# Two feed-forwards' products down in seven block products for each pair of weight chunks, products up in one bank

## The reference

```python
# first block: D_FF = 2816
h = rms_norm(x, ffn_norm_g[l])
g = jnp.einsum('bld,df->blf', h, w_gate[l])
u = jnp.einsum('bld,df->blf', h, w_up[l])
x = x + jnp.einsum('blf,fd->bld', jax.nn.silu(g) * u, w_down[l])
# second block: D_FF_2 = 4096; here the result is normed before it is added to x
relu(h @ w_up_2) ** 2 @ w_down_2
```

## Time and profile before

| | before |
|---|---|
| median of 3 runs | 761.1 us (760.95 to 761.15) |
| profiled execution's span | 759.5 us (mean granted clock 0.997) |
| PE busy | 741.9 us (98%), 4410 matmuls |
| DVE busy | 462.9 us (61%) |
| ACT busy | 373.5 us (49%) |
| POOL busy | 112.7 us (15%) |
| transferred | 130.46 MB, mean 172 GB/s |

### The profile page before, as it was taken

How to read it: one execution, slowest core, us unless ns; L and a number is a source line. 1 busy time by engine, 2 the same in 40 slices (tenths; PEclk the granted TensorE clock), 3 DMA queues, 4 the chain that set the end, 5 groups by cost and what they waited for, 6 DMA issues and landing times.

```text
span 759.5 us, 11083 instructions
## 1 busy us (share of the span) xinstructions
PE 741.9 (98%) x4410; PEld 643.3 (85%) x4410; DVE 462.9 (61%) x643; ACT 373.5 (49%) x535; POOL 112.7 (15%) x138
## 2 busy tenths in 40 slices
PE   6999999999999999999999999999999999999996
PEld 5877778999999999888888888888778899988895
DVE  5898696765555555465746656674848754455433
ACT  6656654654444444275434524663338644344431
POOL 3857540100000000002100000000302111001110
PEclk9999999999999999999999999999999999999998
DMA  9642152786656676355625543474535765655511
GB/s 326 213 127 83 46 173 78 239 285 211 207 188 190 188 227 203 112 174 187 195 84 192 193 139 112 127 262 136 170 102 201 255 197 188 202 187 184 188 45 55
DMA packets 70179, 130.46 MB, mean 172 GB/s; under 512 B 5312, under 2 KB 29072, under 8 KB 70128
## 3 DMA queue, kind: packets, MB, share of 16 engines
q1 hardware_dynamic: 68144, 125.00, 51.8%
q0 software_dynamic: 1552, 4.20, 1.8%
q10 hardware_dynamic: 432, 0.56, 0.2%
HBM read 128.62 MB, written 1.05 MB: 171 GB/s over the span
## 4 chain that ended last, share of the span: by engine, by line
PE 92%; DVE 3%; DMA 2%; issue 1%; ACT 1%; SPq 0%; DVEq 0%; ACTq 0%
PE psum L450 40%; PE psum L885 29%; PE psum L503 11%; PE psum L927 2%; DMA w_raw<-in_w_in 2%; PE psum L677 1%; PE psum L1012 1%; PE psum L598 1%; PE psum L543 1%; PE psum L628 1%; PE psum L1044 1%; DMA w_raw<-in_w_out 1%; PE psum L579 1%; DVE w_lo L1893 1%; PE psum L649 1%
## 5 line engine op out<-in xcount | busy, mean ns | idle before, releaser
L1893 DVE TENSOR_TENSOR w_lo<-w_raw,w_hi 128x1024 fp32r<-128x1024 f32 x225 | 275.3, 1235 | 153.2 <-ACT w_hi L1270 152.5
L1270 ACT ACTIVATE w_hi<-w_raw 128x1024 fp32r<-128x1024 f32 x231 | 241.4, 1059 | 181.3 <-PE psum L885 77.3
L885 PE MATMUL psum<-h_hi,w_hi 128*128 128x256 f32 x608 | 170.3, 284 | 0.6 <-issue 0.6
L885 PE MATMUL psum<-h_hi,w_lo 128*128 128x256 f32 x608 | 169.5, 283 | 0.0
L885 PE MATMUL psum<-h_lo,w_hi 128*128 128x256 f32 x608 | 161.8, 281 | 0.0
L885 PEld LDWEIGHTS psum<-h_hi,w_hi 128*128 128x128 f32 x608 | 114.7, 189 | 1.7 <-issue 0.7
L885 PEld LDWEIGHTS psum<-h_hi,w_lo 128*128 128x128 f32 x608 | 114.4, 188 | 0.0
L885 PEld LDWEIGHTS psum<-h_lo,w_hi 128*128 128x128 f32 x608 | 111.1, 189 | 0.7
L450 PE MATMUL psum<-w_hi,h_hi 128*128 128x512 f32 (+1 forms) x240 | 94.0, 392 | 0.0
L450 PE MATMUL psum<-w_hi,h_lo 128*128 128x512 f32 (+1 forms) x240 | 93.0, 387 | 0.0
L450 PE MATMUL psum<-w_lo,h_hi 128*128 128x512 f32 (+1 forms) x240 | 92.9, 387 | 0.0
(11 more groups left out here) (299 smaller groups left out, 1011.6 us busy)
## 6 DMA issues: line engine op xcount, KB each, us to landing
w_raw<-in_w_in SPq DMA_DIRECT2D x77, 512.0 KB, 4.4
w_raw<-in_w_down SPq DMA_DIRECT2D x54, 512.0 KB, 4.3
w_raw<-in_w_up SPq DMA_DIRECT2D x32, 512.0 KB, 4.2
w_raw<-in_w_gate SPq DMA_DIRECT2D x44, 256.0 KB, 2.9
w_raw<-in_w_up SPq DMA_DIRECT2D x44, 256.0 KB, 3.5
w_raw<-in_w_out SPq DMA_DIRECT2D x16, 512.0 KB, 3.5
w_raw<-in_w_branch_a SPq DMA_DIRECT2D x4, 512.0 KB, 4.2
w_raw<-in_w_branch_b SPq DMA_DIRECT2D x4, 512.0 KB, 4.6
```

Source lines behind the costliest of these rows:

```text
L885: mm = pe.matmul(outs, x[:, cols], y[:, kc, :], start=kc == 0 and n == 0, stop=kc == KC - 1 and n == (1 if i == 0 else 2))
L1270: act.activation(T.w_hi[:, k % SLOTS, :], T.w_raw[:, k % RAW_SLOTS, :], ACT.Copy).then_inc(S.w_rounded, 1)
L1893: dve.tensor_tensor(T.w_lo[:, k % SLOTS, :], T.w_raw[:, k % RAW_SLOTS, :], T.w_hi[:, k % SLOTS, :], ALU.subtract).then_inc(S.w_cut, 1)
```

## The change

Weights down. A pair's weights (two chunks of 128 rows, 1024 columns) are four quarters of 128 x 512, B11, B21 (the rows of the two chunks, left half of the columns) and B12, B22 (right half). The hidden numbers of the pair are four quarters of 128 x 128, A11, A12, A21, A22 (first index the tile of tokens, second the chunk). Instead of eight products of quarters, seven products of sums of quarters are made (Strassen's form in Winograd's variant), each three matmuls of 128x512 that are added up over all pairs in a bank of their own: 21 matmuls a pair in the place of 24. The outputs' four quarters are formed from the seven banks once, at the end. The last pair of each feed-forward is made in the old form, in quarters. FF1 has 11 pairs, FF2 16.

What each pair needs for it:
- POOL makes the sums of the weights: four subtractions of 128x512 (`sum_pair`), and of the hidden numbers: four sums of 128x128 (`sum_hidden`).
- ACT rounds seven quarters of weights (3584 columns in three instructions, before 2048 in two) and seven of hidden numbers (896 columns), DVE cuts as many.
- the pair's weights come in one transfer of 1 MB into one of two buffers, and the next transfer into it waits for the cuts (`load_pair`, in SP's program between the fills).

Weights up. A fill is now one chunk (all 1024 rows, 128 columns; the host lays the arrays out so). The seven product banks leave one bank, so each two groups of 24 matmuls (gate and up of a chunk, or two chunks in FF2) go to the halves of bank 7, and ACT copies the bank out (`take_up`, in FF2 the ReLU in `take_hidden`) before PE goes on with the next two. In FF1 the gate's scaling and the product with the up part now take both operands from SBUF. In PE's order the products down of pair i-2 stand between the products up: three products, gate and up of a chunk, four products, gate and up of the next chunk (FF1); two chunks up, seven products (FF2).

In the diff below unchanged helpers, the memory layout and most of the waits are left out.

```diff
+PRODUCT = {1: (1, 0, 2), 2: (3, 1, 0), 3: (7, 2, 1), 4: (2, 6, 6), 5: (4, 4, 5), 6: (6, 5, 3), 7: (5, 3, 4)}
+EARLY, LATE, LAST = (1, 2, 3), (7, 5, 6, 4), (1, 6, 7, 4, 5, 2, 3)
...
+    def down(q, products, first=False, last=False):
+        buf, i = pair_place(q)
+        pe.wait_ge(S.hidden_cut, q + 1)
+        for n_product, p in enumerate(products):
+            x, y, b = PRODUCT[p]
+            pe.wait_ge(S.pair_cut, pair_parts(q) + NEEDS[p])
...
+            for n, (u, v) in enumerate(((x_hi, y_hi), (x_hi, y_lo), (x_lo, y_hi))):
+                mm = pe.matmul(bank[b][:], u, v, start=first and n == 0, stop=last and n == 2)
...
+    def chunk_up1(j):
+        pe.wait_ge(S.up_taken, j)
+        up_two(W.first["up1", j], 7)
...
+    for i in range(2, PAIRS1):
...
+        down(i - 2, EARLY, first=i == 2)
+        chunk_up1(2 * i)
...
+        down(i - 2, LATE, first=i == 2)
+        chunk_up1(2 * i + 1)
+    down(LAST1 - 1, LAST, last=True)
+    pe.wait_ge(S.up_taken, 2 * PAIRS1)
+    down_quarters(1)
...
+    def round_pair(q, part):
...
+            elif q > 1:
+                act.wait_ge(S.pair_used, pairs_used(q - 1))
+        else:
+            act.wait_ge(S.pair_summed, 4 * pairs_summed(q) + (2 if part == 1 else 4))
...
+    def cut_pair(q, part):
+        buf, i = pair_place(q)
+        dve.wait_ge(S.pair_rounded, pair_parts(q) + part + 1)
+        places, src = ((slice(0, 3), T.pair_raw[i][:, 0:3, :]), (slice(3, 4), T.pair_raw[i][:, 3:4, :]),
+                       (slice(4, 7), T.pair_sums[:]))[part]
+        dve.tensor_tensor(T.pair_lo[buf][:, places, :], src, T.pair_hi[buf][:, places, :], ALU.subtract).then_inc(S.pair_cut, 1)
...
-        dve.tensor_tensor(rows, rows, T.psum[:, b:b + 2, 0:SEQ], ALU.mult).then_inc(S.hidden_done, 1)
+        gate = T.rows[:, j % 2, 0:SEQ]
+        dve.tensor_tensor(gate, gate, T.spread[:], ALU.mult).then_inc(S.gate_scaled, 1)
...
+    def sum_pair(q):
...
+        pool.wait_ge(S.pair_landed[i], pair_loads(q))
+        if q > 0:
+            pool.wait_ge(S.pair_cut, pair_parts(q))
+        pool.tensor_tensor(t1, b12, b11, ALU.subtract).then_inc(S.pair_summed, 1)
+        pool.tensor_tensor(b12, b12, b22, ALU.subtract).then_inc(S.pair_summed, 1)
+        pool.wait_ge(S.pair_summed, 4 * pairs_summed(q) + 1)
+        pool.tensor_tensor(t2, b22, t1, ALU.subtract).then_inc(S.pair_summed, 1)
+        pool.wait_ge(S.pair_summed, 4 * pairs_summed(q) + 3)
+        pool.tensor_tensor(t4, b21, t2, ALU.subtract).then_inc(S.pair_summed, 1)
...
+    def sum_hidden(q, done):
...
+        step(pool.tensor_tensor(s1, a21, a22, ALU.add))
+        pool.tensor_tensor(s3, a21, a11, ALU.subtract)
+        own()
+        step(pool.tensor_tensor(s2, s1, a11, ALU.subtract))
+        own()
+        pool.tensor_tensor(s4, a12, s2, ALU.subtract).then_inc(S.hidden_summed, 1)
```

More of the change, by code:

```diff
@@ L137, in __init__ @@
             self.slab((name, 0), a["w_out"][0][h * WIDE:(h + 1) * WIDE, :], 4, D)
[L138 to L149, removed]
+        for f in range(2 * PAIRS1):
+            self.first["up1", f] = len(self.fills)
+            for w in range(2):
+                self.fills.append([(lambda raw: raw, a["up1"][f, :, w, :])])
         win2 = a["w_in_2"][0]
@@ new lines, in down_quarters @@
+    def down_quarters(block):
+        q = (LAST1, LAST2)[block - 1]
+        buf, i = pair_place(q)
+        pe.wait_ge(S.hidden_cut, q + 1)
+        pe.wait_ge(S.pair_cut, pair_parts(q) + 2)
+        for t, half, b in QUARTER_BANKS[block]:
+            if b != 7:
+                pe.wait_ge(S.formed, 3 * (block - 1) + max(1, b - 2))
+            for c in range(2):
+                y = ((0, 3), (1, 2))[c][half]
+                x_hi, x_lo = T.hid_hi[:, i, 2 * c + t, :], T.hid_lo[:, i, 2 * c + t, :]
+                y_hi, y_lo = T.pair_hi[buf][:, y, :], T.pair_lo[buf][:, y, :]
+                for n, (u, v) in enumerate(((x_hi, y_hi), (x_hi, y_lo), (x_lo, y_hi))):
+                    mm = pe.matmul(bank[b][:], u, v, start=c == 0 and n == 0, stop=c == 1 and n == 2)
+            mm.then_inc(S.quarter_done, 1)
@@ new lines, in square_last @@
+    def square_last(n, t, half, src):
+        act.wait_ge(S.scale_shrunk, 1)
+        act.wait_ge(S.formed, 3 * 2 + n + 1)
+        act.activation(T.rows[:, half, :], src, ACT.Square, scale=T.stat[:, 8 + t:9 + t],
+                       accum_out=T.stat[:, 4 + 2 * t + half:5 + 2 * t + half]).then_inc(S.post_squared, 1)
+    f = W.first["up2", 0]
+    round_to(f + 8)
+    round_pair(FIRST2, 0)
+    take_hidden(0)
+    take_hidden(1)
+    for i in range(2, PAIRS2 + 1):
+        q = FIRST2 + i - 1
+        if i == 2:
+            round_pair(FIRST2, 1)
+            round_pair(FIRST2, 2)
+            round_hidden(FIRST2)
+        if i < PAIRS2:
+            for part in range(3):
+                round_pair(q, part)
+            take_hidden(i)
+            round_to(min(f + 2 * i + 6, len(W.fills)))
+        else:
+            for part in range(2):
+                round_quarters(q, part)
+        round_hidden(q)
@@ L1871, in scalar_program @@
+    copy_first(2)
+    for n, (t, half) in enumerate(((0, 0), (0, 1), (1, 0), (1, 1))):
+        square_last(n, t, half, T.last[t, half])
     act.wait_ge(S.x_posted, 8)
@@ new lines, in vector_program, with form, add_x @@
+    cut_hidden(LAST1)
+    def form(block, n, src, plus, dst):
+        dve.wait_ge(S.product_done, len(PRODUCT) * (block - 1) + n)
+        dve.tensor_tensor(dst, bank[src][:], plus, ALU.add).then_inc(S.formed, 1)
+    p1, u2, u3, u4 = (T.pair_raw[0][:, n, :] for n in range(4))
+    r2 = [T.row_scale[:, 1, t:t + 1] for t in range(TILES)]
+    def add_x(src, t, half):
+        cols = slice(half * WIDE, (half + 1) * WIDE)
+        return dve.scalar_tensor_tensor(T.x[:, t, cols], src, r2[t], T.x[:, t, cols], ALU.mult, ALU.add)
@@ L2401, in vector_program @@
+    step(add_x(bank[1][:], 1, 1))
+    for n, (t, half, b) in enumerate(QUARTER_BANKS[1]):
+        dve.wait_ge(S.quarter_done, n + 1)
+        own()
+        add_x(bank[b][:], t, half).then_inc(S.x_added, 1)
+    cut_pairs("h3", (0, 1), (5, 6), gain(2), T.h_hi, T.h_lo)
+    cut_pairs("h3", (2, 3), (2, 3), gain(2), T.h_hi, T.h_lo)
     r3 = [T.row_scale[:, 2, t:t + 1] for t in range(TILES)]
```

618 lines of the change are left out of this document (407 added, 211 removed).

## The result

The changed kernel takes 821.4 us (821.26 to 822.94, 4 runs) beside 761.0 for the kernel before (760.64 to 761.15, 4 runs): ratio 1.0797, 95% interval 1.0783 to 1.0811. It is 8.0% slower. The prediction was 820 with a range of 786 to 846. The profiled execution has a span of 819.9 us, 60.4 more than before.

A forecast was written before the change was run, and what follows sets the result against it. PE bounds the kernel before; afterwards DVE and POOL taking turns would decide. FF1 +7, FF2 +50 and the end +2 give +59 on the profiled 759.5, thus 818.5, median 820 us, range 786 to 846.

The forecast's parts named there:

- The mechanism: DVE instructions with two SBUF operands and POOL's reading SBUF exclude each other, so their times add up.
- (a): Rival: the lock costs little and PE stays the bound; -12.4 us, 749 us; chance 0.08.
- (b): Rival: the lock holds but fills itself better, FF2's pair 13.2 us; 792 us; chance 0.19.
- FF2: Second feed-forward: DVE and POOL together need 14.3 us a pair against 11.34 before; +50 us.
- late start: FF2's start: PE's first matmuls wait 3 us for fills to be cut, counted inside FF2's +50.
- FF1: First feed-forward: 17.8 us a pair against 17.10 before, plus a longer last chain; +7 us.
- handover: After FF1: the same adds on x as before, so 0, bounds -0.5 to +2 us.
- +6 (pairs): FF1's nine pairs at 0.7 us more each, including a 0.9 us gap for rounding the last sums; +6 us.
- the last chain: Before FF1's last quarters: copy, gate, silu, product, rounding and cut take 5 us beside 4.9 of matmuls; +1 us.
- The end: From the last matmul to the last add's end: 5.3 us where 3.2 were before; +2 us.
- rival (c): PE's clock falls as well during its waits in FF2; +25 us, 845 us; chance 0.12.
- Spared matmuls: Three matmuls of 512 columns fewer a pair in 10 + 15 pairs; 17.4 us of PE time.

The follow-up runs named there:

- two kernels without the lock: Changed kernel with POOL's sums replaced by memsets, or cut to one column: 759.9 us and 764.2 us.
- the frame alone: Changed kernel with eight plain products of quarters a pair (24 matmuls) and no sums: 771.9 us, ratio 1.0147 to the kernel before.
- the kernel with the fills behind: x on DVE plus two earlier starts, and FF1's last half step cuts the next stage's third and fourth fills after the adds on x: 760.4 us.
- the one with the square on ACT: Changed kernel with all eight sums of a pair on DVE and FF2's square moved from POOL to ACT: 766.4 us.
- sums of one column: Changed kernel with POOL's eight sums working on one column only after each block's first pairs: 764.2 us.
- the memsets: Changed kernel with POOL's sums replaced by memsets of about the same length that read nothing: 759.9 us.
- x on DVE: The one with the square on ACT, with POOL's scalings and adds on x after FF1 also moved to DVE: 763.8 us.

## Why the prediction was right, step by step

**The mechanism** was right and is shown: with POOL's reads gone and most of its length kept, 61.5 us go; with its work done by DVE, 44 us. Rivals (a) and (b) are excluded by the pair of 14.06 us.

**FF2**, forecast +50: measured 57.4 - 11.4 = +46.0 from its first product up on, and 3.4 us of late start (11.4 - 8.0), which I had counted inside. Together +49.4. The pair, 14.3 forecast (7.3 + 7.0), is 14.06. Only POOL is without a gap; DVE's one gap of 2.7 us is POOL's last sum and ACT's rounding of it (1.48), beside which POOL has the square and the first small sums.

**FF1**, forecast +7 with no handover: measured +8.0 with it, and the composition was wrong. The pair is 16.94 and not 17.8. I had added a gap of 0.9 us for the rounding before DVE's last cut; in the trace DVE has a fill, the hidden numbers and the cut of 512 columns to do between POOL's last sum (over at 223.4) and this cut (225.98), and its real gap (1.57 us for ACT's copy of bank 7, at 217.3) is filled by POOL. The sum 16.9 of both engines' own work was already the answer. PE's own pair is also 16.24 and not 16.40 (two kernels without the lock show it), because the frame alone takes 0.17 off: 16.93 with 24 matmuls where before had 17.10. What I had missed stands at both ends: the first product down 2.3 us late, waits of 1.3 and 1.4 us before the last quarters, and 4.4 at the handover, which I had at 0 with "the same adds on x as before". They are not the same: before, each quarter had one add; now there are three forms, six adds of parts on DVE, two more as a scaling and an add each on POOL, and four of quarters: 17 instructions for 4. The rows after the last quarters' end near 323.9:

```profile
323.46 0.74 DVE L2641 SCALAR_TENSOR_TENSOR x<-psum,row_scale,x 128x512 f32<-128x512 f32 x1
325.21 3.58 DVE L2641 SCALAR_TENSOR_TENSOR x<-psum,row_scale,x 128x512 f32<-128x512 f32 x5 [1.01 <-POOL x L3269]
```

PE's wait for x before its turns is 3.1 us longer than before, and 1.3 us more pass from there to the first rows, half of it by PE's clock (below).

I had summed +6 (pairs) and +1 (the last chain); measured are -1.4 (pairs), +2.3 (first product down), +2.7 (the last chain) and +4.4 (handover). FF1's total came right because these errors cancel, by luck and not by its terms.

**The end**, forecast +2: the span's end is 3.0 us further behind the last matmul than before, and so is the end of the last add (6.3 for 3.2). Tile 0's two adds (1.41 us) and a scaling stand ahead of tile 1's last sum, which I had counted; the price of the sums that precede them I had not. The kernels whose last products run at the full clock show it whole, 5.3 us (11.1 for 5.8): DVE's first sum for the ends starts 4.0 us ahead of the last matmul's end in the kernel with the fills behind (744.68, 748.65), and 6.3 us ahead in the changed kernel (804.83, 811.09).

**PE's clock**, rival (c): it does fall, at no cost in the pairs but at a cost between them. Granted clock by stretch of the changed kernel:

```profile
610.00:615.00 5.00, 1.77 (x4) 1.48 (x5) 2.33 (x3) 3.79 (x4) 4.92 (x5) 0.60 0.00 0
640.00:645.00 5.00, 3.62 (x18) 3.62 (x19) 4.13 (x3) 3.53 (x5) 4.84 (x6) 0.68 0.19 54
```

After a wait of 4.6 us matmuls of 512 columns follow each other at 0.43 us until 802.0 and then at 0.23:

```profile
798.87 0.80 PE L1018 MATMUL psum<-pair_hi,hidden_hi 128*128 128x512 f32 x1 [4.59 <-DVE hidden_lo L2586]
...
801.59 0.63 PE L1018 MATMUL psum<-pair_hi,hidden_hi 128*128 128x512 f32 x1
802.02 0.48 PE L1018 MATMUL psum<-pair_lo,hidden_hi 128*128 128x512 f32 x1
802.34 0.39 PE L1018 MATMUL psum<-pair_hi,hidden_lo 128*128 128x512 f32 x1
```

Between its waits PE had up to 3 us a pair to spare, and the slower matmuls filled them, as I had argued for pricing it low. At the end, where nothing else is late, it cost: 8 matmuls in 3.47 us (798.87 to 802.34) in place of 8 x 0.2325 = 1.86, 1.6 us. It cost at the handover too, of which the forecast had nothing. The turns of x, in the changed kernel and in the one with the square on ACT:

```profile
326.87 3.33 PE L678 MATMUL psum<-small,x 128*128 128x128 f32 x16 [2.95 <-DVE x L2641]
```

```profile
321.08 2.63 PE L678 MATMUL psum<-small,x 128*128 128x128 f32 x16 [2.92 <-DVE x L2682]
```

In the first the granted clock is 0.50 from 328 to 331, and the next stage's first matmul begins 2.99 us after the first turn; in the second it stays at 1.00, and it is 2.38 us. The next four matmuls then lose 0.6 us more (1.60 us for 1.01), so that some 1.2 us of the handover are the clock's. The waits before were alike, 2.95 and 2.92 us: what decides between the two levels stays open. At FF1's first products down (9 matmuls in 3.72 us for 2.09, after a wait of 2.50) the changed kernel loses nearly nothing, since the two periods from there take 34.2 us and two of its pairs 33.9; the kernel with sums of one column, whose pairs PE bounds, loses it all.

**Spared matmuls**, 17.4 us: confirmed where PE bounds. Kernels with 24 and with 21 matmuls a pair differ by 0.69 and 0.68 in the two blocks, 3 x 0.2325 = 0.70. The form pays only once POOL does none of it, and then most of the 17 us go to FF1's and FF2's starts, the handover and the end.

The Trainium skill, "SBUF — State Buffer", Who interferes with whom, has the rule that decided this, contention with a GpSimd instruction that reads SBUF and not with one that only writes it; the memsets at 0.95 us beside cuts of 1.76 agree that what does not read SBUF passes.

## What to carry to other kernels

Before work goes to an idle engine, ask if it can run while its neighbour works: DVE with two SBUF operands and POOL reading SBUF take turns, so their times add, and work moved from PE to POOL here cost 8%. If the sum of both is over PE's time, give the sums to DVE itself, where one of 128x512 took 0.69 us as logged, and POOL's first, begun while DVE was idle, 1.29. Then count what a cheaper form adds outside its loop: the instructions between the last matmul and the next stage are paid nearly in full, and letting the matrix engine accumulate in open banks spared 3.7 us of them here.

## What the runs showed of the hardware that I had not expected

- POOL's memsets to SBUF run beside DVE's cuts with both at their own length (954 ns for 128x1024; 1758 for DVE's 1536 columns), while a POOL instruction that reads one number a partition takes 0.19 us with DVE idle and 1.18 us with DVE in a cut.
- Most kernels bound by PE scatter more from run to run (763.4 to 767.6, 759.8 to 764.3) than the kernel bound by the lock (821.3 to 822.9). The time goes with the mean granted clock: of the eight runs with x on DVE, the three at 0.981 to 0.983 took 766.8 to 768.3 us, the five at 0.986 to 0.990 762.4 to 764.4. Why the clock differs from run to run stays open.
